# A two-layer recurrent decoder trunk: ScalarE rounds the weights of two input projections, two first tiles and two first chunks start in another order

## The chip, the cores and the metric

One NeuronCore of a Trainium2 chip runs the whole program. The metric is the device time of one execution in microseconds. Engines are called PE (TensorE), DVE (VectorE), ACT (ScalarE), POOL (GpSimd) and SP (SyncE, which here only issues DMAs).

## The reference

576 token columns (512 of a prompt, 8 samples of 8) pass through two layers with shared weights, all in float32, width 1024:

```python
h = rms_norm(x, norm_mix[l])
y, s = even_mixer(h, ...)  if l % 2 == 0 else odd_mixer(h, ...)   # z = h @ w_in ... y = concat @ w_out
x = x + y
h = rms_norm(x, norm_ffn[l])
y, c = conv_ffn(h, ...)          # u = h @ w_up; causal conv of 3; (val * silu(gate)) @ w_down
x = x + y
```

The even mixer projects to 30 tiles of 128 columns (16 for an mLSTM, 14 for an RWKV-7) and 8 gate columns; the odd mixer to 16 tiles (12 for gated linear attention, 4 for an S5 scan) and 16 gate columns. The feed-forward part has 44 tiles up and 22 x 128 rows down. Outputs are both token groups and all new states.

## The kernel before

**How a projection is computed.** Activations stay transposed, eight tiles k of 128 x 576. Every matrix product in float32 is made of three passes with operands rounded to the fast float32 format: high x high, high x low, low x high (`mm3`). A tile of output is 8 k x 2 halves of 288 columns x 3 passes = 48 matmuls. So each weight tile (128 x 1024) that a DMA brings into one of the two slots of `w_ring` has to be split: `w_hi` = rounded weight, `w_lo` = weight minus `w_hi`, both with two slots. A slot may be refilled with tile t+2 once PE has finished tile t (`proj_done`), and PE may start tile t+2 once it is split (`w_split`) and its PSUM pair has been read out (`FREE`). SP loads tile t+2 into `w_ring` when tile t is split.

**Who splits.** In both input projections (`e_in`, `o_in`), both output projections and both down projections POOL does both steps (`chunk`, L1327: a multiplication by ones, then a subtraction). In the two up projections (`ffn`) ACT makes the high half (L1962) and POOL only the subtraction. The activations are split by ACT (high, L1924) and DVE (low, L270 called from `low_sum`), with squares for the norm beside them, in `split_x`.

**Start.** PE computes the 36 gate columns (`small`) as each split tile k of x arrives, then the sum of squares over partitions (`norm`), then tile 0 of `e_in`. `norm` releases ACT's Ln and Exp that make `rstd`; every read-out of a tile (`evac`, `to_ext`, on DVE) multiplies by it. After `rstd`, ACT works on the gate rows (L2001 to L2005) and one exponential for the S5 part (L2007, its step size). DVE interleaves read-outs of tiles 0 to 15 with gate logs, running maxima, row logs and, after tile 5, `s5_angles` (both the sine and the cosine argument), after tile 7 `s5_coefficients`.

**Odd layer.** In `odd_dve` DVE reads out tiles 0 and 1, then for t = 0, 1 computes log decays, a scan and key differences (L1013 to L1020), and only then reads out tiles 2 and 3. In `odd_act` ACT does the gate functions; then, for 14 level masks, DVE's differences, ACT's Exp and DVE's scalings follow each other (`levels`), between the read-outs of tiles 4 to 15.

**Feed-forward.** Per tile: read-out by DVE, three conv taps (ACT, DVE, DVE), SiLU, product, high half, low half. POOL copies conv state in and out (`state_in`, `state_out`). `down` has, per output tile, three chunks of 8, 7 and 7 k in alternating slots. PE's first chunk (8 k) needs 14 low halves of the activations (`act_lo`), the second 15 and the third all 22. Before its first chunk POOL copies out the last conv state (it waits for the read-out of up tile 43) and, in layer 0, splits the 16 gate columns of the next layer (`wad`).

Each engine executes its instructions in the order written; the code order is the schedule.

Of the kernel before, what the change touches and what calls it, by code (L numbers as in the profile page):

```python
# [26 lines left out]
P = 128  # L27
# [4 lines left out]
TH = T // 2  # L32
# [143 lines left out]
def program(nc, d, o):  # L176

    ctx = ExitStack()
    with ctx:
# [702 lines left out]
        def odd_act(act, A, chain, norm, head_norm, split_h):  # L882
            norm(2)

# [19 lines left out]
            level_exps(0, 14)  # L904
# [64 lines left out]
        def odd_dve(dve, V, chain, evac, head_norm, split_h):  # L969
# [40 lines left out]
            for t in range(2):  # L1010
# [4 lines left out]
                chain(V.tensor_tensor_scan(b_, c_("scan128", T), la, 0.0, ALU.mult, ALU.add))  # L1015
                kd = KG[:, t, :]
# [4 lines left out]
            evac_z(2)  # L1021
            diffs(0)
            diffs(1)
            evac_z(3)
# [298 lines left out]
        def _(pool):  # L1323
# [22 lines left out]

            def ffn(l):
# [35 lines left out]
                for t in range(2 * FT):  # L1383
# [3 lines left out]
                    if t + 2 < 2 * FT:  # L1387
                        state_in(t + 2)

            def down(l):  # L1390
                pool.wait_ge(S("proj_done"), USE[f"down{l}"] - 1)
                pool.wait_ge(S("w_split"), CHUNK0[f"down{l}"])
                with pool.Fori(0, 4) as i:
                    chain.loop(i, 6)
# [8 lines left out]
                    chain.end_loop(4)  # L1403
# [17 lines left out]
            ffn(0)  # L1421
            pool.wait_ge(S("o_small_in"), 32)
            split(wad, wad_hi, wad_lo, S("small_split"))
            down(0)
            pool.wait_ge(S("chunk_used"), 17)
            project("o_in")
            pool.wait_ge(S("s5_y"), SP4)
            project("o_out")
            ffn(1)
            down(1)  # L1430
# [3 lines left out]
        def _(pe):  # L1434
# [7 lines left out]
            def small(name, out, hi, lo):  # L1442

                for k in range(KT):
# [5 lines left out]
                last.then_inc(S("gates_done"), 1)  # L1450

            def project(name, between=None, breaks=(), lead=0):
# [15 lines left out]
                for s in () if lead else range(2):  # L1468
# [443 lines left out]
        def _(act):  # L1912
            A = nc.scalar.activation
            chain = Chain(act, S("act_chain"))

            def split_x(n, name):

                for k in range(KT):
# [11 lines left out]
                    A(sq[:, k % 2, :], xT[:, k, :], ACT.Square).then_inc(S("sq_ready"), 1)  # L1930

# [926 lines left out]
```

## Time and profile before

| | us |
|---|---|
| median of 3 runs | 1760.52 (1759.35 to 1769.03) |
| span of the profiled execution | 1763.6 |
| PE busy | 1634.1 (93%) |
| DVE / POOL / ACT busy | 1053.1 / 875.7 / 471.8 |
| PE idle between matmuls, waiting for DVE arena L267 | 26.1 |
| ... for DVE hT_r L270 (low halves of x) | 18.2 |
| ... for POOL dual_r L267 (a split weight) | 16.2 |

The given time of an execution is that of the whole device run; of the profiled one only the span, 1763.6 us from its first to its last instruction, is given, and it lies 3.1 us above the median. `PE PP L280` is any matmul, `L267` any two-input elementwise operation, `L270` any scalar_tensor_tensor: these are helper lines, so what an instruction is has to be read from its tiles and its place. A start and a duration stand at the head of a timeline row, in brackets the idle time of its engine just before it and what ended it. Matmuls overlap, so their durations (0.29 at full clock, 0.43 at half) are longer than the distance of their starts.

### The profile page before, as it was taken

How to read it: one execution, taken by the hardware profiler on the slowest of the kernel's cores; microseconds unless marked ns; L12 is line 12 of the kernel's file. 1: busy time of each engine (PE TensorE's matmuls, PEld its weight loads, DVE VectorE, ACT ScalarE, POOL GpSimd, SP SyncE). 2: the span in 40 equal slices, each digit the busy share in tenths (PEclk: the TensorE clock that was granted, in tenths of full speed). 3: DMA queues.
4: the chain of work that ended last, by engine and by line, in shares of the span. 5: the costliest groups of instructions: out<-in, count | busy, mean ns of one | idle time of the engine just before them, and what ended most of it. 6: DMA issues, size and time to landing. Idle time of an engine off the chain costs nothing. (4 is left out here: it accounts for less than half of the span.)

```text
span 1763.6 us, 35383 instructions
## 1 busy us (share of the span) xinstructions
PE 1634.1 (93%) x14910; PEld 1576.0 (89%) x14910; DVE 1053.1 (60%) x1533; ACT 471.8 (27%) x688; POOL 875.7 (50%) x731
## 2 busy tenths in 40 slices
PE   6999996588998999999989998999899999998996
PEld 5999985487987999999989998977799999998996
DVE  4816768747645777776632239676676777765012
ACT  4002123610133343333310031132414333332001
POOL 4666688094013644444376656700374444445763
PEclk8999988688999999999999999998999999999998
DMA  4222111021052222222222222274332222222222
GB/s 176 84 71 83 60 74 54 1 75 56 13 200 69 90 84 83 83 83 83 72 66 88 76 79 60 71 210 139 91 98 77 84 83 83 84 83 61 81 83 88
DMA packets 50679, 149.09 MB, mean 85 GB/s; under 512 B 17552, under 2 KB 19232, under 8 KB 48416
## 3 DMA queue, kind: packets, MB, share of 16 engines
q1 hardware_dynamic: 50592, 147.91, 26.3%
q8 instruction: 58, 0.95, 0.2%
q14 instruction: 29, 0.24, 0.0%
HBM read 127.58 MB, written 19.13 MB: 83 GB/s over the span
## 5 line engine op out<-in xcount | busy, mean ns | idle before, releaser
L280 PE MATMUL PP<-arena_r,dual_r 128*128 128x288 f32 (+1 forms) x6428 | 1116.9, 298 | 39.9 <-POOL dual_r L267 16.2
L280 PEld LDWEIGHTS PP<-arena_r,dual_r 128*128 128x128 f32 (+1 forms) x6428 | 965.3, 190 | 44.3 <-POOL dual_r L267 13.9
L280 PE MATMUL PP<-hT_r,dual_r 128*128 128x288 f32 (+1 forms) x2176 | 647.7, 298 | 0.0
L267 POOL TENSOR_TENSOR dual_r<-w_ring,dual_r 128x1024 fp32r<-128x1024 f32 (+1 forms) x198 | 485.1, 2450 | 17.7 <-ACT dual_r L1962 4.6
L267 POOL TENSOR_TENSOR dual_r<-w_ring,cst 128x1024 fp32r<-128x1024 f32 (+1 forms) x114 | 216.7, 1901 | 408.6 <-PE PP L280 262.2
L280 PEld LDWEIGHTS PP<-hT_r,dual_r 128*128 128x128 f32 (+1 forms) x2176 | 410.5, 189 | 1.3
L270 DVE SCALAR_TENSOR_TENSOR rowbuf<-rowbuf,convp 128x592 f32<-128x592 f32 x176 | 271.3, 1542 | 91.3 <-ACT rowbuf L1985 90.7
L280 PE MATMUL PP<-arena 64*64 64x64 f32 (+6 forms) x3640 | 206.0, 256 | 37.1 <-DVE arena L267 15.3
L280 PEld LDWEIGHTS PP<-arena 64*64 64x64 f32 (+2 forms) x3640 | 182.8, 148 | 57.9 <-issue 32.6
L1962 ACT ACTIVATE dual_r<-w_ring 128x1024 fp32r<-128x1024 f32 x84 | 89.2, 1062 | 332.1 <-PE PP L280 332.1
L267 DVE TENSOR_TENSOR xT<-PP,xT 128x576 f32<-128x576 f32 x32 | 24.2, 758 | 255.5 <-PE PP L280 255.5
L267 DVE TENSOR_TENSOR rowbuf<-PP,rstd 128x288 f32<-128x288 f32 (+2 forms) x306 | 90.5, 351 | 109.0 <-PE PP L280 97.6
L267 DVE TENSOR_TENSOR arena<-arena 128x256 f32<-128x256 f32 (+12 forms) x168 | 128.9, 800 | 6.9 <-ACT arena L1953 3.7
L280 PE MATMUL PP<-rowbuf_r,dual_r 128*128 128x288 f32 (+1 forms) x544 | 112.4, 301 | 7.0 <-DVE arena L267 6.3
L1365 POOL COPY rowbuf<-arena 128x16 f32<-128x16 f32 x88 | 19.7, 226 | 173.4 <-DVE rowbuf L270 173.4
L280 PEld LDWEIGHTS PP<-rowbuf_r,dual_r 128*128 128x128 f32 (+1 forms) x544 | 88.4, 189 | 9.1 <-DVE arena L267 6.5
L1372 POOL COPY arena<-rowbuf 128x18 f32<-128x18 f32 x88 | 17.6, 200 | 139.0 <-DVE rowbuf L267 139.0
L1985 ACT ACTIVATE rowbuf<-rowbuf,convp 128x592 f32<-128x592 f32 x88 | 76.4, 868 | 24.8 <-DVE rowbuf L267 24.8
L267 DVE TENSOR_TENSOR arena<-PP,rstd 128x576 f32<-128x576 f32 (+2 forms) x28 | 21.1, 753 | 88.5 <-PE PP L280 78.7
L267 DVE TENSOR_TENSOR rstd<-rstd,sq 128x576 f32<-128x576 f32 x35 | 73.2, 2091 | 0.1
L267 DVE TENSOR_TENSOR arena<-arena,PP 128x128 f32<-128x128 f32 (+4 forms) x114 | 35.3, 311 | 50.9 <-PE PP L280 41.4
L280 PE MATMUL PP<-dual_r 128*128 128x288 f32 (+1 forms) x244 | 58.9, 297 | 1.9 <-DVE hT_r L270 1.9
(266 smaller groups left out, 1348.9 us busy)
## 6 DMA issues: line engine op xcount, KB each, us to landing
w_ring<-in_w SPq DMA_DIRECT2D x150, 512.0 KB, 3.5
w_ring<-in_w_down SPq DMA_DIRECT2D x32, 448.0 KB, 3.3
w_ring<-in_w_down SPq DMA_DIRECT2D x16, 512.0 KB, 3.5
xT<-in_x SPq DMA_DIRECT2D x8, 576.0 KB, 7.1
gy_scratch<-dual SPq DMA_DIRECT2D x1, 2304.0 KB, 7.0
dual<-gy_scratch SPq DMA_DIRECT2D x1, 2304.0 KB, 13.7
out_y<-hT SPq DMA_DIRECT2D x4, 576.0 KB
xT<-in_C SPq DMA_DIRECT2D x1, 2064.0 KB, 9.2
```

The lines of the kernel that those rows point to most:

```text
L267: return eng.tensor_tensor(out, a, b, op)
L270: return nc.vector.scalar_tensor_tensor(out=out, in0=a, scalar=s, in1=b, op0=op0, op1=op1)
L280: return nc.tensor.matmul(out, lhsT, rhs, start=start, stop=stop)
L1365: G.tensor_copy(samp[:, :, 0:2], convin[:, t, :].rearrange("p (j n) -> p j n", j=8)).then_inc(S("conv_in"), 1)
L1372: G.tensor_copy(convout[:, t, :].rearrange("p (j n) -> p j n", j=9), last2).then_inc(S("conv_out"), 1)
L1962: A(w_hi[:, t % 2, :], w_ring[:, t % 2, :], ACT.Copy).then_inc(S("w_hi"), 1)
L1985: A(cv[:, i % 2, s, 0:NCV - 2], ext[:, s, 0:NCV - 2], ACT.Identity, bias=convp[:, l, p0 + 3:p0 + 4], scale=convp[:, l, p0:p0 + 1]).then_in ...
```

## The change

The whole change, by place:

- **Start.** POOL no longer makes the high halves of weight tiles 0 and 1; ACT does, after the squares of x tiles 5 and 6. PE computes the gate columns for k = 0 to 4, then waits for tile 0's split and computes tile 0 for k = 0 to 4, then alternates gate columns and tile 0 for k = 5, 6, 7, then `norm`.
- **ScalarE's high halves.** For `e_in` (all 30 tiles) and `o_in` (tiles 2 to 15) ACT copies `w_ring` to `w_hi` (`high`) and POOL only subtracts (`project_low`). The calls to `high` are placed in ACT's order: tiles 2 to 9 after the S5 step exponential, 10 to 13 after the sines, and so on.
- **Moved orders.** `s5_angles` in two parts, after tiles 5 and 6. In the odd layer the read-outs of tiles 2 and 3 move into the gate loop, between scan and key differences; ACT does both Exp before both Ln. POOL starts the first chunk of `down` before the last conv state is copied out, and splits `wad` between chunks 1 and 2.

```diff
-        def odd_act(act, A, chain, norm, head_norm, split_h):
+        def odd_act(act, A, chain, norm, high, head_norm, split_h):
             norm(2)
+            high("o_in", "o_hi", 2)
...
             for t in range(2):
-                chain(A(BC[:, t, :], BC[:, t, :], ACT.Exp, scale=-1.0))
+                last = A(BC[:, t, :], BC[:, t, :], ACT.Exp, scale=-1.0)
+            chain(last)
+            for t in range(2):
                 A(BC[:, t, :], BC[:, t, :], ACT.Ln, bias=1.0).then_inc(S("gl_sp"), 1)
+            high("o_in", "o_hi", 3)
             for t in range(2):
+                high("o_in", "o_hi", 4 + t)
                 act.wait_ge(S("gl_kd"), t + 1)
...
-            level_exps(0, 14)
+            for k0, k1, js in ((0, 2, (6,)), (2, 4, (7,)), (4, 6, (8,)), (6, 8, (9,)), (8, 9, (10, 11, 12, 13)),
+                               (9, 11, (14,)), (11, 13, (15,)), (13, 14, ())):
+                level_exps(k0, k1)
+                for j in js:
+                    high("o_in", "o_hi", j)
...
                 chain(V.tensor_tensor_scan(b_, c_("scan128", T), la, 0.0, ALU.mult, ALU.add))
+                evac_z(2 + t)
                 kd = KG[:, t, :]
...
-            evac_z(2)
             diffs(0)
             diffs(1)
-            evac_z(3)
...
+            def project_low(name, sem, ahead=0):
+                first_chunks = 2
+                if name == "o_in":
+                    for s in range(first_chunks):
+                        pool.wait_ge(WL[s], 16 * (CHUNK0[name] // 2 + 1))
+                        pool.wait_ge(S("proj_done"), USE[name] + s - 1)
+                        chunk(s)
+                with pool.Fori(1, RUNS[name][1] // 2) as i:
+                    for s in range(2):
+                        pool.wait_ge(S(sem), 2 * i + (s - 1 + ahead))
+                        tt(G, w_lo[:, s, :], w_ring[:, s, :], w_hi[:, s, :], ALU.subtract).then_inc(S("w_split"), 1)
...
-                for t in range(2 * FT):
+                for t in range(2 * FT - 1):
                     state_out(t)
...
+                return lambda: state_out(2 * FT - 1)
-            def down(l):
+            def down(l, last_state, between=None):
+                c0 = CHUNK0[f"down{l}"]
                 pool.wait_ge(S("proj_done"), USE[f"down{l}"] - 1)
-                pool.wait_ge(S("w_split"), CHUNK0[f"down{l}"])
-                with pool.Fori(0, 4) as i:
-                    chain.loop(i, 6)
+                for e in range(6):
+                    tile, j = e // 3, e % 3
+                    pool.wait_ge(WL[e % 2], 16 * (c0 // 2 + e // 2 + 1))
+                    if e == 2 and between is not None:
+                        between()
+                    if e == 1:
+                        last_state()
+                        pool.wait_ge(S("proj_done"), USE[f"down{l}"])
+                    elif j == 1:
+                        pool.wait_ge(S("proj_done"), USE[f"down{l}"] + tile)
+                    elif e:
+                        pool.wait_ge(S("chunk_used"), 16 * l + 2 * tile + (j == 2) + 1)
+                    chunk(e % 2, DCH[j][1] * P)
+                with pool.Fori(1, 4) as i:
...
-            for s in range(2):
-                pool.wait_ge(WL[s], 16)
-                chunk(s)
-            project("e_in", 1)
+            for s in range(2):
+                pool.wait_ge(S("e_hi"), s + 1)
+                tt(G, w_lo[:, s, :], w_ring[:, s, :], w_hi[:, s, :], ALU.subtract).then_inc(S("w_split"), 1)
+            project_low("e_in", "e_hi", 2)
...
+            def first_tile(ks):
+                for k in ks:
+                    pe.wait_ge(S("h_lo"), k + 1)
+                    c = slice(k * P, (k + 1) * P)
+                    for a in range(2):
+                        h = slice(a * TH, (a + 1) * TH)
+                        last = mm3(PP[0][:, a, 0:TH], w_hi[:, 0, c], w_lo[:, 0, c], H_HI["e_in"][k][:, h],
+                                   H_LO["e_in"][k][:, h], k == 0, k == KT - 1)
+                if ks[-1] == KT - 1:
+                    last.then_inc(S("proj_done"), 1)
...
-            small("e_in", PP[2][0:36], wif_hi, wif_lo)
+            small("e_in", PP[2][0:36], wif_hi, wif_lo, range(5))
+            pe.wait_ge(S("w_split"), 1)
+            pe.wait_ge(FREE[0], 1)
+            first_tile(range(5))
+            for k in range(5, KT):
+                small("e_in", PP[2][0:36], wif_hi, wif_lo, range(k, k + 1))
+                first_tile(range(k, k + 1))
             norm(0)
-            project("e_in", None, {11: mlstm_columns})
+            project("e_in", None, {11: mlstm_columns}, done=1)
...
+            def high(name, sem, j):
+                act.wait_ge(WL[j % 2], 16 * ((CHUNK0[name] + j) // 2 + 1))
+                if USE[name] + j >= 2:
+                    act.wait_ge(S("proj_done"), USE[name] + j - 1)
+                A(w_hi[:, j % 2, :], w_ring[:, j % 2, :], ACT.Copy).then_inc(S(sem), 1)
...
                     A(sq[:, k % 2, :], xT[:, k, :], ACT.Square).then_inc(S("sq_ready"), 1)
+                    if n == 0 and k in (5, 6):
+                        high("e_in", "e_hi", k - 5)
...
             A(t_s, l_st, ACT.Exp).then_inc(S("s5_trig"), 1)
+            for j in range(2, 10):
+                high("e_in", "e_hi", j)
             act.wait_ge(S("o_rows"), 1)
...
             A(t_c, t_c, ACT.Sin).then_inc(S("s5_trig"), 1)
+            for j in range(10, 14):
+                high("e_in", "e_hi", j)
             for j in range(12, 16):
+                high("e_in", "e_hi", j + 2)
...
             for k in range(14):
                 s = k % 2
+                if k < 12:
+                    high("e_in", "e_hi", 18 + k)
...
-                    if j == 5:
-                        s5_angles()
+                    if j in (5, 6):
+                        s5_angles(j - 5)
```

## Rows read from the trace of the kernel before

**Rows 1.** The page's table of engines: busy time, share of the span, instructions.
```profile
PE 1634.1 (93%) x14910; PEld 1576.0 (89%) x14910; DVE 1053.1 (60%) x1533; ACT 471.8 (27%) x688; POOL 875.7 (50%) x731
```
**Rows 2.** PE's waits by releaser: us in total, times, longest.
```profile
PE PP L280 <- DVE arena L267: 26.1, 8, 7.0
PE PP L280 <- DVE hT_r L270: 18.2, 7, 8.5
PE PP L280 <- POOL dual_r L267: 16.2, 4, 7.4
```
**Rows 3.** Timeline of the start, 0 to 40 us: splits, their rivals, and PE's restarts.
```profile
11.57 0.81 DVE L270 SCALAR_TENSOR_TENSOR hT_r<-xT,vec,arena_r 128x576 fp32r<-128x576 f32 x1
12.68 2.13 POOL L267 TENSOR_TENSOR dual_r<-w_ring,cst 128x1024 fp32r<-128x1024 f32 x1 [5.01 <-DMA w_ring<-in_w]
12.97 2.45 DVE L270 SCALAR_TENSOR_TENSOR hT_r<-xT,vec,arena_r 128x576 fp32r<-128x576 f32 x1
20.67 0.45 PE L280 MATMUL PP<-arena_r,dual_r 128*36 128x288 f32 x1 [3.54 <-DVE hT_r L270]
25.51 0.75 DVE L267 TENSOR_TENSOR rstd<-rstd,sq 128x576 f32<-128x576 f32 x1
29.17 0.65 ACT L1935 ACTIVATE rstd<-PP 128x576 f32<-128x576 f32 x1 [3.69 <-PE PP L280]
39.01 0.23 ACT L2007 ACTIVATE rowbuf<-rowbuf 128x32 f32<-128x32 f32 x1
41.95 0.76 DVE L267 TENSOR_TENSOR arena<-PP,rstd 128x576 f32<-128x576 f32 x1 [5.64 <-PE PP L280]
48.32 0.76 DVE L267 TENSOR_TENSOR arena<-PP,rstd 128x576 f32<-128x576 f32 x1 [5.60 <-PE PP L280]
```
**Rows 4.** Stretches: PE, PEld, DVE, ACT, POOL busy (instructions), PE clock, DMA share, GB/s.
```profile
15.40:21.90 6.50, 2.88 (x12) 1.80 (x12) 6.50 (x4) 1.35 (x2) 6.42 (x3) 0.50 0.77 285
83.20:91.40 8.20, 8.14 (x50) 8.15 (x51) 4.50 (x19) 2.52 (x4) 1.75 (x1) 0.79 0.21 64
1075.60:1084.30 8.70, 8.69 (x50) 8.69 (x51) 5.02 (x14) 1.84 (x4) 0.00 (x0) 0.74 0.21 61
889.30:897.30 8.00, 7.91 (x49) 7.91 (x50) 8.00 (x8) 3.14 (x6) 4.77 (x3) 0.80 0.42 122
```
**Rows 5.** The two steps of a weight split on POOL, and ACT's high half.
```profile
35.60 1.90 POOL L267 TENSOR_TENSOR dual_r<-w_ring,cst 128x1024 fp32r<-128x1024 f32 x1 [12.76 <-PE PP L280]
37.57 2.40 POOL L267 TENSOR_TENSOR dual_r<-w_ring,dual_r 128x1024 fp32r<-128x1024 f32 x1
L1962 ACT ACTIVATE dual_r<-w_ring x84: 1057/1062/1063, 606.0 to 1586.4; 128x1024 fp32r<-128x1024 f32 x84
```
**Rows 6.** Timeline around PE's stop before tile 8 of the even layer.
```profile
82.46 1.41 DVE L270 SCALAR_TENSOR_TENSOR arena<-PP,rstd 128x576 f32<-128x576 f32 x2
83.25 0.43 PE L280 MATMUL PP<-arena_r,dual_r 128*128 128x288 f32 x1 [2.80 <-DVE arena L270]
```
**Rows 7.** Timeline of the odd layer's input projection: DVE, and PE's restart at tile 4.
```profile
1063.20 4.62 DVE L267 TENSOR_TENSOR arena<-arena 128x512 f32<-128x512 f32 x2
1075.61 0.61 PE L280 MATMUL PP<-rowbuf_r,dual_r 128*128 128x288 f32 x1 [6.30 <-DVE arena L267]
1100.06 8.40 DVE L267 TENSOR_TENSOR arena<-arena 128x288 f32<-128x288 f32 x8
1148.95 0.82 DVE L267 TENSOR_TENSOR arena<-arena 128x288 f32<-128x288 f32 x2
```
**Rows 8.** Timeline between up and down projection, layer 0, and PE's restart in layer 1.
```profile
883.90 3.22 DVE L270 SCALAR_TENSOR_TENSOR rowbuf<-rowbuf,convp 128x592 f32<-128x592 f32 x2 [0.95 <-ACT rowbuf L1985]
891.43 8.83 DVE L267 TENSOR_TENSOR arena_r<-arena,arena_r 128x576 fp32r<-128x576 f32 x8
889.39 110.86 PE L280 MATMUL PP<-arena_r,dual_r 128*128 128x288 f32 x819 [7.36 <-POOL dual_r L267]
1605.24 142.84 PE L280 MATMUL PP<-arena_r,dual_r 128*128 128x288 f32 x1056 [6.11 <-POOL dual_r L267]
```

More of the change, by code:

```diff
@@ L1402, in down @@
                         chunk(e % 2, DCH[j][1] * P)
[L1403 removed]
+                    chain.end_loop(3)
             pool.sem_inc(S("chunk_used"), 1)
@@ L1420, in _, with small_weights @@
             project("e_out")
[L1421 to L1424, printed above, removed]
+            last_state = ffn(0)
+            def small_weights():
+                pool.wait_ge(S("o_small_in"), 32)
+                split(wad, wad_hi, wad_lo, S("small_split"))
+            down(0, last_state, small_weights)
             pool.wait_ge(S("chunk_used"), 17)
-            project("o_in")
+            project_low("o_in", "o_hi")
             pool.wait_ge(S("s5_y"), SP4)
             project("o_out")
-            ffn(1)
-            down(1)
+            down(1, ffn(1))
         @block.tensor
@@ L1440, in norm, with small @@
                 last.then_inc(S("sq_summed"), 1)
-            def small(name, out, hi, lo):
-                for k in range(KT):
+            def small(name, out, hi, lo, ks=range(KT)):
+                for k in ks:
                     pe.wait_ge(S("h_lo"), 8 * SPLIT[name] + k + 1)
@@ L1449, in small, with project @@
                                    k == 0, k == KT - 1)
-                last.then_inc(S("gates_done"), 1)
-            def project(name, between=None, breaks=(), lead=0):
+                if ks[-1] == KT - 1:
+                    last.then_inc(S("gates_done"), 1)
+            def first_tile(ks):
+                for k in ks:
+                    pe.wait_ge(S("h_lo"), k + 1)
[4 more added lines that the diff above has]
+                                   H_LO["e_in"][k][:, h], k == 0, k == KT - 1)
+                if ks[-1] == KT - 1:
+                    last.then_inc(S("proj_done"), 1)
+            def project(name, between=None, breaks=(), lead=0, done=0):
                 n = RUNS[name][1]
@@ L1467, in project @@
                             last.then_inc(S("proj_done"), 1)
-                for s in () if lead else range(2):
+                for s in () if lead else range(done, 2):
                     pe.wait_ge(S("w_split"), CHUNK0[name] + s + 1)
@@ L2210, in _ @@
             split_x(2, "o_in")
-            odd_act(act, A, chain, norm, head_norm, split_h)
+            odd_act(act, A, chain, norm, high, head_norm, split_h)
             split_x(3, "ffn1")
@@ L2367, in row_logs, with s5_angles @@
                 V.tensor_copy(r_mo[:, 1:9], m_s).then_inc(S("ml_rows"), 1)
-            def s5_angles():
-                dve.wait_ge(S("s5_trig"), 1)
-                chain(tt(V, t_a, l_re, t_s, ALU.mult))
-                chain(tt(V, t_b, l_im, t_s, ALU.mult))
-                for out, shift in ((t_s, 0.0), (t_c, np.pi / 2)):
+            def s5_angles(part):
+                if part == 0:
+                    dve.wait_ge(S("s5_trig"), 1)
+                    chain(tt(V, t_a, l_re, t_s, ALU.mult))
+                    chain(tt(V, t_b, l_im, t_s, ALU.mult))
+                for out, shift in (((t_s, 0.0),) if part == 0 else ((t_c, np.pi / 2),)):
                     chain(V.tensor_scalar(t_n, t_b, 1.0 / TWO_PI, shift / TWO_PI, ALU.mult, ALU.add))
```

1 line of the change is left out of this document (added).

## The prediction

> **What bounds the kernel now.** First the table of engines: PE is busy 93% of the span, the others at most 60% [rows 1]. So time is saved only where PE stands idle or runs at the lower of its two clock levels. Second, PE's waits by releaser: only three groups have to do with what is edited, DVE's read-outs and masks (26.1 us), the low halves of x (18.2) and split weights from POOL (16.2) [rows 2]. Third, the timeline around each restart, which gives the places: the start, tile 8 of the even layer (2.80 us idle), tile 4 of the odd layer (6.30), and the first chunk of either down projection (7.36 and 6.11) [rows 3, 6 to 8]. Fourth, the granted clock of the stretch behind each restart: a tile that needs 6.37 us in steady state (read-outs at 41.95 and 48.32, [rows 3]) takes 8.1 to 8.7 us behind a stop, at a mean clock of 0.74 to 0.80 [rows 4]. A stop therefore costs its idle time and about 1.9 us more.
>
> A tile's split is 1.90 + 2.40 us on POOL [rows 5], below 6.37, so in steady state it is hidden before and after. With ACT's 1.06 for the high half, the path from a finished tile to the split becomes 1.06 + 2.40 = 3.5 us instead of 4.3: worth nothing by itself. ACT must get to it in time, though: everything queued ahead of it in ACT's order now stands ahead of PE's tile.
>
> **POOL and DVE.** A low half of x takes DVE 0.81 us; the one at 12.97, issued behind POOL's 2.13 us at 12.68, took 2.45 and ended 0.6 us after POOL did [rows 3]. DVE is held until POOL's instruction ends. Read-outs from PSUM stay at 0.76 with POOL at work. The Trainium skill, "SBUF — State Buffer", section "Who interferes with whom", says the same: two SBUF inputs on DVE and a reading GpSimd instruction exclude each other for the whole instruction, one SBUF input does not. By that rule an earlier POOL chunk only moves DVE's delay; without it both down projections would gain their whole idle time. The trace agrees with the rule.
>
> **The start.** POOL's first instruction on weights now waits for ACT. ACT needs 1.3 to 1.4 us per k; high half 0 falls at about 14.2 to 15.3, POOL subtracts until 18.0 (2.75 us with DVE beside it), high half 1 until 17.8, POOL until 20.6. DVE is held for two POOL instructions instead of four: the last square is summed at about 22.6 instead of 26.3 (25.51 + 0.75, [rows 3]). PE has computed gates 0 to 4 by 15, idles until 18.0, and is at half clock then, as between 15.4 and 21.9 now [rows 4]. It has 30 + 36 matmuls left, 0.133 us apart at full clock (6.37 / 48), 0.24 at half. At half clock for about 4 us (some 17), then 49 x 0.133: it ends at 28.6, `norm` behind it. ACT's Ln starts at about 29.8 against 29.17 [rows 3]: the gates are no earlier, but tile 0 is finished too, a full tile ahead.
>
> What is late next is tile 2. Its high half stands behind the gate rows and the S5 exponential: that ends at 39.24 now [rows 3], some 39.9 then. Plus 1.06 and 2.40: split at 43.4. Tile 1 ends at about 36, so PE idles over 7 us and starts tile 2 at 43.4; before it started at 41.9, when tile 1 was finished. So +1.5 us, and +1.9 for the lower clock: the gain is given back, **+3.4**. Bounds: tile 2 released at once by ACT would be a tile early, -6; a walk wholly at half clock (66 x 0.24 = 16 us) makes the chain 5 us later, +9.
>
> **s5_angles in two.** Read-out 6 came at 82.46, behind both parts, and PE waited 2.80 for it [rows 6], plus 1.9 clock: **-4.7**. With half of it behind tile 7, and PE 3.4 us later anyway, both read-outs fall within their 6.4 us. The coefficients now wait on ACT (high half 9, a table load, the sines) and push read-out 8 by 3 us at most, still within a tile. Even layer: -1.3. Later highs stand one per tile beside a read-out; the squares after tile 25 (3 us) fit too. POOL reaches the S5 work up to 1 us earlier; I cost that at 0, +-1.5.
>
> **Odd layer.** Tile 4 waited 6.30 us because read-out 2 stood behind both scans and key differences (4.62 of the latter were mostly POOL's hold) [rows 7]; the tile then took 8.7 at clock 0.74 [rows 4]. After the move read-out 2 follows the first scan, at 1063, just as tile 2 ends; read-out 3 at 1069.3. High halves 4 and 5 are ready at tile end + 3.5. PE goes on without a stop: 6.30 + 8.7 - 6.4 = **-8.6**. DVE is then about 2 us behind PE instead of ahead; its next cover is POOL's shorter turn. Eight mask operations took 8.40 us with POOL in the way and would take 4 x 0.82 = 3.3 free [rows 7]; with one 2.4 hold per tile, 5.7 + 0.75, just PE's pace. High halves 7, 8, 9 come behind mask exponentials and keep, by this account, 1 to 2.5 us of slack. The saved table loads on ACT are hidden behind tile 1. Bounds: 0 if the lag grows into new stops, -8.6 - 1.
>
> **Down projections.** Layer 0: chunk 0 is split from 876.9 to 881.3, before tile 43 ends at 882.0: the 7.36 stop goes. What is late next is the second chunk: it needs `act_lo` 15, and that comes by DVE, two taps (3.22), ACT's SiLU, the product, then the low halves (from 891.43, 8.83 for eight) [rows 8]. Now POOL's chunk 0 holds tile 42's taps and delays read-out 43 by 1 us, chunk 1 (884.3 to 888.5) holds the taps, chunk 2 the product. I get the 15th low half at 894.6. PE has finished chunk 0 by 888.4, stops 6.2 us, and runs chunk 1 partly at half clock until 902.1; it ended at 902.9 before (897.3 + 42 x 0.133). **-0.9**. Layer 1, without the gate split: **-1.1**. Bounds for both together: 0, and, if DVE were not held, 7.36 + 6.11 + 2 x 1.7 = -17.
>
> **Sum.** +3.4 - 4.7 - 8.6 - 0.9 - 1.1 = -11.9 on the span of 1763.6. The span lies 3.1 above the median of the runs; the same difference on 1760.5 gives **1748.6 us**.
>
> **Rivals.**
> A. *The down projections gain most of their stop* (low halves come in time). For: the first chunk's wait is truly on POOL. Against: the chain of holds above. Another -7: 1741.5.
> B. *Half of the odd layer's gain is eaten by new small stops.* For: slack of 1 us at high halves 8 and 9. Against: POOL's hold per tile falls from 4.3 to 2.4. +4.5: 1753.
> C. *The start is worse*: PE stays at half clock, since the walk starts from idle. +5: 1753.5.
> D. *Slower: high halves late in ACT's queue.* In the odd layer each stands behind Exps that wait for DVE's differences, which are held by POOL. Should DVE lag 2 us more than I find, highs 7, 8, 9, 14 and 15 are each 2 us late, each with 1.9 us of lower clock: 5 x 3.9 = 19.5, hence 1768. It decides from a DVE lag of about 4 us at tile 6. Against: before, with POOL's longer turns, DVE caught up by tile 9.
>
> **Chances.** Forecast 0.55 (own range 1744 to 1752), A 0.15, B 0.13, C 0.10, D 0.04, others 0.03. A measurement of this kernel can tell about 0.5% (8.8 us) from no change. Faster by more: the forecast but for its upper edge (0.52), A, and a few of B and C (0.07): 0.74. Within: 0.22. Slower: 0.04. Range 1739 to 1755.
>
> **What the profile after would show.** PE idle 6 to 8 us before tile 2 of the even layer, released by POOL, with ACT's gate rows ahead of the high half; no stop at tile 8; none at tile 4 of the odd layer, input projection there 8 to 9 us shorter; in both down projections the stop moved behind 48 matmuls, released by DVE's `arena_r`, 5 to 6 us long. Wrong if tile 2 starts before 42, if the stop before the second chunk is absent, or if new stops appear among odd tiles 7 to 15.

## The result, and the profile after

The changed kernel takes 1752.2 us (median of 7 runs, 1749.19 to 1757.59) against 1766.7 for the kernel before on the same chip (7 runs, 1758.65 to 1769.03). The ratio is 0.9939 [0.9920, 0.9957]: 0.61% or some 11 us faster. (The two medians lie 14.4 us apart, because the seven runs before fall into three at 1758.65 to 1760.52 and four at 1766.65 to 1769.03; the two means lie 11.1 us apart.) The interval reaches from 0.43% to 0.80%, across the 0.5% mark, so a gain of more than 0.5%, to which the prediction gave 0.74, is likely but not shown. The forecast, 1748.6 from a base of 1760.5, was a gain of 0.68%; 1752.2 lies in its range. The size was nearly right. Two of the reasons were not, as the experiments show.

The after page's engine table, to be read beside [rows 1]: PE's share is still 93%, VectorE is busy 1009.9 us and POOL 785.8, and ScalarE has taken over part of POOL's work.

```profile
PE 1629.8 (93%) x14910; PEld 1573.0 (90%) x14910; DVE 1009.9 (58%) x1533; ACT 513.0 (29%) x730; POOL 785.8 (45%) x687
```

PE's waits by releaser (what PE waited for: us in total, times, longest) answer to [rows 2]:

```profile
PE PP L280 <- DVE arena L267: 19.4, 7, 6.8
PE PP L280 <- POOL dual_r L267: 13.3, 4, 7.2
PE PP L280 <- DVE arena_r L267: 12.5, 3, 6.4
PE PP L280 <- DVE hT_r L270: 11.4, 5, 8.8
```

DVE's `arena` fell from 26.1 mostly by the 6.3 of the odd layer's tile 4, and the 2.8 of L270 (tile 8, even layer) is gone. `hT_r` fell from 18.2. POOL's 16.2 became 13.3, but with other contents: the two stops before the down projections (7.36 and 6.11, [rows 8]) left the group, and stops at the start came in (3.30 and 7.22). The down stops now stand as `arena_r`, up from 1.9 to 12.5. These are the three restarts in the timeline of PE (start, us, instruction, count, idle before and its releaser), at tile 0, at tile 2 and in the first down projection:

```profile
18.37 0.51 PE L280 MATMUL PP<-arena_r,dual_r 128*128 128x288 f32 x1 [3.30 <-POOL dual_r L267]
...
43.49 0.60 PE L280 MATMUL PP<-arena_r,dual_r 128*128 128x288 f32 x1 [7.22 <-POOL dual_r L267]
...
890.79 4.42 PE L280 MATMUL PP<-arena_r,dual_r 128*128 128x288 f32 x17 [6.36 <-DVE arena_r L267]
```

The stretches behind them, in the windows view (window, its length, busy us and count of PE, PEld, DVE, ACT, POOL, then granted clock, DMA share, GB/s): tile 2 of the even layer runs at a clock of 0.65, then tiles 3 to 8 of the even layer and the first tiles of the odd one at 1.00 without a gap.

```profile
43.00:52.00 9.00, 8.51 (x44) 8.52 (x45) 0.00 (x0) 0.00 (x0) 2.68 (x2) 0.65 0.39 117
52.70:92.00 39.30, 39.30 (x298) 39.30 (x298) 29.78 (x63) 9.16 (x11) 14.59 (x6) 1.00 0.27 81
1051.00:1071.80 20.80, 20.80 (x160) 20.80 (x159) 19.46 (x26) 9.10 (x11) 7.92 (x4) 1.00 0.26 77
```

The same two stretches of the kernel before, cut at the same read-outs:

```profile
48.30:91.40 43.10, 40.16 (x290) 39.72 (x290) 37.89 (x62) 3.14 (x5) 27.49 (x12) 0.96 0.26 82
1056.60:1084.30 27.70, 21.40 (x147) 21.17 (x146) 23.77 (x26) 5.73 (x8) 14.64 (x6) 0.88 0.20 58
```

The row to look at is POOL's: 27.49 us and 12 instructions became 14.59 and 6, and DVE, with one more instruction, is busy 29.78 us instead of 37.89. DVE's work did not shrink; the time for which its instructions were held did.

To compare kernels whose early parts shift all later ones, every profile was cut at the starts of the same VectorE read-outs. The first column is when the gate columns are read out, the first use of `rstd`; "to tile 2" goes from there to read-out 2; "up to down" goes from the read-out of the last up tile to the first read-out of the down projection. In us, granted clock in brackets:

| kernel | rstd read | to tile 2 | tiles 2 to 9 | odd tiles 1 to 15 | up to down, layer 0 | layer 1 |
|---|---|---|---|---|---|---|
| before | 31.9 | 16.4 (1.00) | 49.5 (0.97) | 97.5 | 26.6 | 25.7 |
| after | 32.7 | 20.1 (0.74) | 44.5 (1.00) | 88.95 | 25.5 | 23.8 |
| change | +0.8 | +3.7 | -5.0 | -8.6 | -1.1 | -1.9 |

That is 12.1 us. The two spans (1763.6 and 1747.4) differ by 16.2. Between the even layer's last read-out and the first read-out of its output projection (231.19 to 555.55 in before), where nothing is edited, after needs 317.9 us and before 324.4; the profiles of the twelve other kernels have 318.4 to 326.7 for the same work. And one stretch in the even layer went the other way by 3.0 (last section). So profile against profile overstates the change, and the stages are needed to see it. The stages scatter too: seven kernels (after, e1, e2, e4, e5, e9, e10) have the same down projections, and in their profiles the layer 0 stretch takes 25.2 to 25.6 us, the layer 1 stretch 23.8 (after) to 25.0 (e10). Against before that is -0.7 to -1.9 for layer 1, so the -1.9 of the table lies at the favourable end.

### The profile page after: what moved, and what is told of

It reads as the page before. It is cut to its first block, busy times and chain, and to the rows that moved or that the text cites. A ratio compares the mean times of both kernels' runs of the same rounds, so it can differ in the third digit from the quotient of the medians.

```text
span 1747.4 us, 35327 instructions
## 1 busy us (share of the span) xinstructions
PE 1629.8 (93%) x14910; PEld 1573.0 (90%) x14910; DVE 1009.9 (58%) x1533; ACT 513.0 (29%) x730; POOL 785.8 (45%) x687
## 4 chain that ended last, share of the span: by engine, by line
PE 82%; DVE 8%; issue 4%; ACT 2%; DMA 1%; POOL 1%; SPq 1%; DVEq 0%; ACTq 0%; POOLq 0%
PE PP L280 82%; DVE arena L267 3%; POOL dual_r L267 1%; DVE xT L267 1%; DMA w_ring<-in_w 1%; DVE rowbuf L270 1%; SPq L538 1%; DVE rstd L267 1%; DVE arena L270 0%; DVE hT_r L270 0%; DVE hT L267 0%; DMA y_scratch<-arena 0%; DVE hT L270 0%; PE PP L1744 0%; ACT arena L2237 0%
## 5 line engine op out<-in xcount | busy, mean ns | idle before, releaser
L280 PE MATMUL PP<-arena_r,dual_r 128*128 128x288 f32 (+1 forms) x6428 | 1118.6, 298 | 39.8 <-POOL dual_r L267 13.3
L270 DVE SCALAR_TENSOR_TENSOR rowbuf<-rowbuf,convp 128x592 f32<-128x592 f32 x176 | 273.7, 1555 | 91.4 <-ACT rowbuf L2049 90.7
L267 POOL TENSOR_TENSOR dual_r<-w_ring,cst 128x1024 fp32r<-128x1024 f32 (+1 forms) x70 | 127.9, 1828 | 291.4 <-PE PP L280 147.5
L280 PEld LDWEIGHTS PP<-arena 64*64 64x64 f32 (+2 forms) x3640 | 179.3, 146 | 57.5 <-issue 30.9
L2026 ACT ACTIVATE dual_r<-w_ring 128x1024 fp32r<-128x1024 f32 x84 | 89.2, 1062 | 332.1 <-PE PP L280 332.1
L267 DVE TENSOR_TENSOR arena<-arena 128x256 f32<-128x256 f32 (+12 forms) x168 | 109.2, 684 | 7.3 <-ACT arena L2017 3.7
L1976 ACT ACTIVATE dual_r<-w_ring 128x1024 fp32r<-128x1024 f32 x44 | 46.6, 1060 | 166.9 <-PE PP L280 166.9
```

The lines of the kernel that those rows point to most:

```text
L267: return eng.tensor_tensor(out, a, b, op)
L270: return nc.vector.scalar_tensor_tensor(out=out, in0=a, scalar=s, in1=b, op0=op0, op1=op1)
L280: return nc.tensor.matmul(out, lhsT, rhs, start=start, stop=stop)
L1976: A(w_hi[:, j % 2, :], w_ring[:, j % 2, :], ACT.Copy).then_inc(S(sem), 1)
L2026: A(w_hi[:, t % 2, :], w_ring[:, t % 2, :], ACT.Copy).then_inc(S("w_hi"), 1)
```

## The experiments

The prediction's account takes ScalarE's high halves as worth nothing by themselves and gives the gains in both input projections to the moved orders. The other account: the gains come from ScalarE's high halves, because VectorE is then held by one POOL instruction per tile instead of two. All times are medians and all ratios are to the kernel before on the same chip.

**e1: the walk undone.** Gates, sum of squares and tile 0 one after another again, all else as after.

```diff
-            first_tile(range(5))
-            for k in range(5, KT):
-                small(..., range(k, k + 1))
-                first_tile(range(k, k + 1))
-            norm(0)
-            project("e_in", None, {11: mlstm_columns}, done=1)
+            small("e_in", PP[2][0:36], wif_hi, wif_lo, range(KT))
+            norm(0)
+            project("e_in", None, {11: mlstm_columns})
```

> The changed kernel with TensorE's first instructions put back in the old order: all gate columns, the norm, then tile 0 alone; ScalarE's high halves stay. My theory: the walk over k is worth nothing, because tile 2 waits for its high half, which stands in ScalarE's queue behind the gate rows. In the old order the gate columns end at about 23 us and the norm at 24.5, some 5 us EARLIER than with the walk, so ScalarE ends its exponential for S5 at about 35 instead of 40.0 and tile 2's split is ready at about 38.4 instead of 43.5; tiles 0 and 1 fill TensorE from 24.5 to 39 (partly at half clock). Tile 2 then starts at 38 to 40, 4 to 5 us earlier than in the changed kernel: about 1748 us, 3 to 6 below it. Rival (the walk pays by itself, a tile of work placed into idle time): tile 2 starts 4 to 6 us later than 43.5, 1757.

1747.7 us, 0.9909 [0.9889, 0.9929]. Read-out 2 falls at 46.05 instead of 52.74: the walk costs 6.7 us at this place. ScalarE's queue and PE, from e1's timeline:

```profile
25.75 0.66 ACT L1993 ACTIVATE rstd<-PP 128x576 f32<-128x576 f32 x1 [6.01 <-PE PP L280]
...
35.74 1.04 ACT L1970 ACTIVATE dual_r<-w_ring 128x1024 fp32r<-128x1024 f32 x1
...
39.39 0.40 PE L280 MATMUL PP<-arena_r,dual_r 128*128 128x288 f32 x1 [0.72 <-POOL dual_r L267]
```

And in the kernel after:

```profile
29.92 0.65 ACT L1999 ACTIVATE rstd<-PP 128x576 f32<-128x576 f32 x1 [9.79 <-PE PP L280]
...
39.76 0.23 ACT L2071 ACTIVATE rowbuf<-rowbuf 128x32 f32<-128x32 f32 x1
39.89 1.99 ACT L1976 ACTIVATE dual_r<-w_ring 128x1024 fp32r<-128x1024 f32 x2
```

With the walk, `norm` comes behind tile 0, so ScalarE's Ln, its gate rows and then high half 2 all come 4 us later (39.89 against 35.74), and PE idles 7.22 us before tile 2 instead of 0.72. Without it the start is 2.3 us shorter than before (46.05 against 48.32 in [rows 3]).

**e2: both angle parts together again**, after tile 5.

```diff
-                    if j in (5, 6):
-                        s5_angles(j - 5)
+                    if j == 5:
+                        s5_angles(0)
+                        s5_angles(1)
```

> The changed kernel with both parts of the S5 angles behind tile 5 again. Theory: the split of the angles is worth nothing in the changed kernel, since tile 2 is late and everything behind it with it, and since GpSimd holds VectorE for half as long: read-out 6 ends at about 82 to 83, tile 8 is due at 84.5, no stop, 0 +- 1 us against the changed kernel in the stretch up to tile 9 (read-out 9 at 97.3 in both). Rival (my prediction's row for it): the stop of 2.8 us before tile 8 and 1.9 us of lower clock come back, read-out 9 at about 102.

1749.71 us, 0.9916 [0.9893, 0.9939]. Tiles 2 to 9 take 44.5 us at clock 1.00, as in after. Splitting the angles is worth nothing at this place; the 5.0 us there come from something else. Here tile 2 is late, though, which gives VectorE slack; e9 tests the same without that.

**e3: the moved read-outs alone**, on the kernel before (`evac_z` of tiles 2 and 3 inside the gate loop).

```diff
                 ...   # scan of gate t
+                evac_z(2 + t)
                 ...   # key differences of gate t
-            evac_z(2)
-            evac_z(3)
```

> The kernel before with only the read-outs of odd tiles 2 and 3 moved into the gate loop; GpSimd still makes both halves. Theory: the move alone removes the stop before tile 4 (6.3 + 2.3 us), the high halves on ScalarE have no part in it: the stretch from odd tile 1 to tile 15 shortens by 8 to 9 us, total -8.6 us or 0.5%. Rival: without ScalarE's high halves GpSimd holds VectorE twice per tile, the lag at the masks grows beyond a tile, and new stops at tiles 8 to 10 take back 3 to 8 us: total -1 to -5 us.

1759.4 us, 0.9992 [0.997, 1.0013], no difference that can be measured. In the trace odd tiles 1 to 15 take 94.2 us instead of 97.5: -3.3, not the -8.6 expected; the rival's -1 to -5 holds. Two stops are left among them, the longer of 3.5 us. PE's waits in that stretch (1020 to 1160 us):

```profile
PE PP L280 <- DVE arena L267: 4.0, 2, 3.5
```

**e4: the down projection's new order on POOL alone**, on the kernel before: chunk 0 before the last conv state, `wad` between chunks 1 and 2.

```diff
-                pool.wait_ge(S("w_split"), CHUNK0[f"down{l}"])
-                with pool.Fori(0, 4) as i:
+                for e in range(6):
+                    ...
+                    if e == 1:
+                        last_state()
+                        ...
+                    chunk(e % 2, DCH[j][1] * P)
+                with pool.Fori(1, 4) as i:
```

> The kernel before with only GpSimd's new order at the start of both down projections. Theory: the stop moves from the first chunk to the second, which waits for low halves of the activations: from the last up tile's read-out to the first read-out of the down projection 1 to 2 us less in each layer, total -2 to -3 us, hardly measurable. Rival: both stops go, -13 to -17 us.

1763.14 us, 1.0 [0.9984, 1.0015]. In its trace the stretches are 25.3 and 24.8 instead of 26.6 and 25.7, -1.3 and -0.9: near the predicted -0.9 and -1.1, and together too small for the runs to tell.

**e5: high halves 2 and 3 moved ahead** in ScalarE's order: 2 before the Ln that makes `rstd`, 3 before the gates' Ln.

```diff
+            high("e_in", "e_hi", 2)
             ...   # rstd
+            high("e_in", "e_hi", 3)
             ...   # gate rows
-            for j in range(2, 10):
+            for j in range(4, 10):
```

> The changed kernel with ScalarE's high half of tile 2 moved ahead of the norm's Ln (ScalarE idles there) and that of tile 3 ahead of the gates' Ln. Theory: tile 2's split was late only by its place in ScalarE's order. Tile 2 now starts right behind tile 1 at about 36.5 instead of 43.5 and at full clock, tile 3 waits up to 1.5 us: 8 to 10 us less at read-out 9, provided VectorE's row logs keep pace; total 1742 to 1745 us. Rival: VectorE's chain of gate and row logs becomes the bound (its 17 us of work between read-outs 2 and 5 start earlier by only part of it) and 3 us or less remain.

1744.37 us, 0.9897 [0.9878, 0.9915]. ScalarE's rows:

```profile
29.62 1.06 ACT L1976 ACTIVATE dual_r<-w_ring 128x1024 fp32r<-128x1024 f32 x1 [10.78 <-PE PP L280]
...
31.99 0.65 ACT L1999 ACTIVATE rstd<-PP 128x576 f32<-128x576 f32 x1
...
38.55 1.06 ACT L1976 ACTIVATE dual_r<-w_ring 128x1024 fp32r<-128x1024 f32 x1
```

The Ln that makes `rstd` is 2.1 us later than in after, since high half 2 (which has to wait for tile 0's buffer) stands ahead of it. Yet tile 2 is read out at 43.28, 9.5 us earlier than in after: the stop of 7.22 us and the half clock behind it are gone. The time came out as expected (1742 to 1745). What held the walk back was a place in ScalarE's queue. Tile 2 is also 2.8 us ahead of e1's; the high halves moved without the walk were not run, so what the walk itself is worth with them is open.

**e6: POOL hardly splits the first three chunks of the down projections**, so that next to nothing holds VectorE there. It leaves out the split of all but 16 columns of each of these chunks.

```diff
-                    chunk(e % 2, DCH[j][1] * P)
+                    chunk(e % 2, 16 if e < 3 else DCH[j][1] * P)
```

> Leaves out nearly all of the weight split of the first three chunks of both down projections (16 of 1024 or 896 columns are split), otherwise the changed kernel. Theory: GpSimd's splits hold VectorE and so delay the low halves that the second chunk waits for. Without them the 15th low half comes at read-out 43 plus 0.9 (ScalarE's tap) + 1.6 (two taps) + 0.7 (SiLU) + 1.0 (product) + 0.75, about 6 us behind the end of the up projection instead of 12: the first chunk (6.4 us) covers it and the stop before the second chunk vanishes (0 to 0.5 us instead of 6.3), 6 to 8 us less per layer. Rival: the chain of VectorE and ScalarE sets the stop by itself: it stays above 4 us.

1735.64 us, 0.9876 [0.9835, 0.9917]. Both stretches take 17.6 us at clock 1.00, -7.9 and -6.2 against after. VectorE's rows between up and down, in after:

```profile
880.73 4.25 DVE L270 SCALAR_TENSOR_TENSOR rowbuf<-rowbuf,convp 128x592 f32<-128x592 f32 x2 [0.95 <-ACT rowbuf L2049]
...
885.75 4.23 DVE L267 TENSOR_TENSOR arena<-rowbuf 128x512 f32<-128x512 f32 x2 [0.76 <-ACT rowbuf L2031]
...
889.90 5.42 DVE L267 TENSOR_TENSOR arena_r<-arena,arena_r 128x576 fp32r<-128x576 f32 x8
```

and in e6:

```profile
883.21 1.80 DVE L270 SCALAR_TENSOR_TENSOR rowbuf<-rowbuf,convp 128x592 f32<-128x592 f32 x2 [0.95 <-ACT rowbuf L2049]
...
885.78 0.83 DVE L267 TENSOR_TENSOR arena<-rowbuf 128x512 f32<-128x512 f32 x2 [0.77 <-ACT rowbuf L2031]
...
886.52 5.47 DVE L267 TENSOR_TENSOR arena_r<-arena,arena_r 128x576 fp32r<-128x576 f32 x8
```

Two taps take 1.80 instead of 4.25, the two products 0.83 instead of 4.23, the eight low halves the same 5.4: in after POOL's chunks 1 and 2 lie over the taps and the products, and the low halves come behind them. Nothing was taken from PE's or ScalarE's work, and the stop before the second chunk is gone: it came from the hold.

**e7: PE waits per k in the last chunk of the first tile**, and that chunk is the larger one.

```diff
-DCH = ((0, 8), (8, 7), (15, 7))
+DCH = ((0, 7), (7, 7), (14, 8))
 ...
+                                    if a == 0 and k0 + nk > AHEAD and k > k0:
+                                        pe.wait_ge(S("act_lo"), FT * l + k + 1)
```

> The changed kernel with down chunks of 7, 7 and 8 k instead of 8, 7, 7, and with TensorE waiting for each low half k by itself in the third chunk. Theory: only the last 8 activations are late; two chunks (11.2 us) now need none of them, and the third can start with the 15th low half: no stop of 6 us, per layer 4 to 6 us less, total about 1742. Rival: the low halves are so late that TensorE trails them one by one and loses the same time at half clock: less than 1 us per layer.

1748.89 us, 0.9926 [0.9908, 0.9943]. Layer 0's stretch is 24.3 us (after 25.5), layer 1's 23.9 (23.8). One long stop became two short ones, and PE then kept running:

```profile
894.62 0.64 PE L280 MATMUL PP<-arena_r,dual_r 128*128 128x288 f32 x3 [2.58 <-DVE arena_r L267]
897.08 9.19 PE L280 MATMUL PP<-arena_r,dual_r 128*128 128x288 f32 x55 [1.83 <-DVE arena_r L267]
```

The idle time falls by some 2 us and the stretch by 1.2 at most, as the rival had it; 4 to 6 us per layer had been expected. The eight low halves, 5.42 us in after, take longer here, because POOL's next splits now lie over them:

```profile
892.20 8.84 DVE L267 TENSOR_TENSOR arena_r<-arena,arena_r 128x576 fp32r<-128x576 f32 x8
```

**e8: e5 and e7 together.**

```diff
 # e5's high halves 2 and 3, and e7's DCH and waits per k
```

> The two improvements of this call together (early high halves of tiles 2 and 3; down chunks 7, 7, 8 with a wait per k). They lie in different stretches, so they add: 1732 to 1738 us, 1.6% below the kernel before. If both rivals hold: within 4 us of the changed kernel.

1740.05 us, 0.9879 [0.9856, 0.9902]. Read-out 2 comes at 43.6, the down stretches are 24.7 and 24.1 us, against 25.5 and 24.8 in e5's profile. The 1732 to 1738 expected were missed, since e7's part brought less than 1 us per layer instead of 4 to 6.

**e9: e5 with the angles together**, a test of e2's answer where PE is 9 us earlier and read-outs have less slack.

```diff
 # e5's high halves 2 and 3, and e2's s5_angles(0); s5_angles(1) after tile 5
```

> e5 (tiles 2 and 3 split early, TensorE some 9 us ahead of the changed kernel) with both parts of the S5 angles behind tile 5 again. Theory: splitting the angles counts once the start is not late. VectorE's chain behind read-out 2 (gate logs, maxima, row logs, angles) then has no slack of 9 us: read-out 6 comes 2 to 5 us behind its tile's due time and tile 8 stops: the stretch from read-out 2 to read-out 9 takes 47 to 50 us instead of 44.5. Rival: GpSimd's shorter hold alone (one instruction per tile instead of two) frees VectorE, and the stretch stays at 44.5: the split of the angles is worth nothing anywhere.

1744.77 us, 0.9892 [0.987, 0.9915], like e5's 0.9897. Tiles 2 to 9 take 44.5 again, not the 47 to 50 expected: the rival holds. VectorE's read-outs about the angles, which are both done between 62.60 and 68.2:

```profile
61.93 0.74 DVE L270 SCALAR_TENSOR_TENSOR arena<-PP,rstd 128x576 f32<-128x576 f32 x1
...
68.16 0.75 DVE L270 SCALAR_TENSOR_TENSOR arena<-PP,rstd 128x576 f32<-128x576 f32 x1
...
74.04 0.76 DVE L270 SCALAR_TENSOR_TENSOR arena<-PP,rstd 128x576 f32<-128x576 f32 x1 [5.13 <-PE PP L280]
```

Both parts fit between two read-outs 6.2 us apart, and at the next one VectorE waits 5.13 us for PE. Before, the read-out behind them came at 82.46 and kept PE waiting 2.80 us [rows 6]. What the hold costs is seen on five small VectorE products just ahead of the angles. In before, where both POOL instructions of a tile lie over them (67.51 to 72.76):

```profile
67.38 5.53 DVE L267 TENSOR_TENSOR arena<-arena 4x512 f32<-4x512 f32 x5
```

and in e9, where no POOL instruction does:

```profile
60.23 1.63 DVE L267 TENSOR_TENSOR arena<-arena 4x512 f32<-4x512 f32 x5
```

Of what is edited in this stretch, the split angles are out of account by e2 and e9, and the late tile 2 by e9. That leaves ScalarE's high halves. They were not run alone on the kernel before, so this is by elimination.

**e10: the read-outs moved back**, in the kernel after: ScalarE's high halves without the move. This and e3 are the two halves of the odd layer's change.

```diff
-                evac_z(2 + t)
+            evac_z(2)
             ...   # key differences of gate 1
+            evac_z(3)
```

> The changed kernel with the read-outs of odd tiles 2 and 3 behind the gate loop again, ScalarE's high halves kept. Read-out 1 to 15 took 97.5 us before, 88.9 in the changed kernel, 94.2 with the move alone. Theory: the shorter hold makes the gate loop about 3 us shorter, but read-out 2 still stands behind it and behind ScalarE's exponentials' inputs; tile 4 stops for 3 to 5 us and runs at half clock: 94 to 96 us, so the two edits give 1.5 to 4 and 3.3, and together more than their sum. There is one more danger: the high half of tile 4 and 5 stand ahead of the key exponentials, which wait for nothing new. Rival: ScalarE's high halves alone bring the whole gain: 89 to 90 us.

1753.01 us, 0.994 [0.9919, 0.9961], the ratio of after (0.9939). Odd tiles 1 to 15 take 88.9 us, which is after's own number (before 97.5, e3 94.2); 94 to 96 were expected, and the rival's 89 to 90 holds. Its windows row has no gap and full clock:

```profile
1052.00:1073.00 21.00, 21.00 (x161) 21.00 (x160) 17.88 (x24) 8.50 (x12) 8.32 (x3) 1.00 0.21 57
```

VectorE's timeline, in the order of before:

```profile
1056.28 2.54 DVE L1023 TENSOR_SCALAR arena<-arena 128x576 f32<-128x576 f32 x1
...
1060.24 0.83 DVE L267 TENSOR_TENSOR arena<-arena 128x512 f32<-128x512 f32 x2
...
1061.77 0.46 DVE L1023 TENSOR_SCALAR arena<-arena 128x576 f32<-128x576 f32 x1
...
1063.66 2.84 DVE L267 TENSOR_TENSOR arena<-arena 128x512 f32<-128x512 f32 x2
1066.43 0.74 DVE L267 TENSOR_TENSOR arena<-PP,rstd 128x576 f32<-128x576 f32 x1
```

The first pair of key differences, 4.62 us in [rows 7], takes 0.83, the second 2.84, and read-out 2 follows at 1066.43, in time for tile 4, which before was released by it with 6.30 us lost. From read-out 1 to read-out 2 VectorE works through the same instructions in 11.6 us here and in 18.2 before. In neither trace does it wait for ScalarE on the way, so the other edit left in e10, both Exp ahead of both Ln, is not what made this faster. In after, with the move, read-out 2 stands ahead of the key differences, and VectorE waited 1.04 us for PE there; that is slack which tile 4 does not need:

```profile
1057.47 0.76 DVE L267 TENSOR_TENSOR arena<-PP,rstd 128x576 f32<-128x576 f32 x1 [1.04 <-PE PP L280]
1058.15 3.01 DVE L267 TENSOR_TENSOR arena<-arena 128x512 f32<-128x512 f32 x2
```

**e11: ScalarE also makes the high halves of the down projections' first two chunks** (on e5); POOL only subtracts there.

```diff
+                    if e < 2:
+                        pool.wait_ge(S("w_hi"), 2 * FT * l + 2 * FT - 1 + e)
+                        tt(G, w_lo[:, e, 0:m], w_ring[:, e, 0:m], w_hi[:, e, 0:m], ALU.subtract)
+                        continue
 ...
+                    A(w_hi[:, t % 2, 0:m], w_ring[:, t % 2, 0:m], ACT.Copy)   # for t = 44, 45 too
```

> e5 and, in both down projections, the high halves of the first two chunks made by ScalarE, as it does for the up tiles; GpSimd only subtracts there. Theory (VectorE's hold sets the stop before the second chunk): two of GpSimd's instructions fall away that stood before VectorE's taps and product, so the 15th low half comes some 4 us earlier, the stop falls from 5.5 to 6.4 us to 2 to 3, and each layer gains 3 to 5 us: total about 1736 to 1738, 7 below e5. Rival: the third chunk, which needs all 22 low halves and whose two instructions still hold VectorE, takes the gain back: 0 to 2 us per layer.

1750.21 us (1750.05 without one execution of 3149 us, see the last section), 0.9917 [0.9898, 0.9936]; its down stretches are 27.2 and 27.4 us, 1.7 and 2.6 worse than e5's.

```profile
874.44 12.70 DVE L267 TENSOR_TENSOR arena_r<-arena,arena_r 128x576 fp32r<-128x576 f32 x8
...
881.31 2.40 POOL L267 TENSOR_TENSOR dual_r<-w_ring,cst 128x1024 fp32r<-128x1024 f32 x1 [1.97 <-PE PP L280]
...
887.28 7.99 PE L280 MATMUL PP<-arena_r,dual_r 128*128 128x288 f32 x42 [6.12 <-DVE arena_r L267]
```

The taps and products are less held, but POOL, done sooner, starts its next split while the eight low halves run: these take 12.70 us instead of 5.42, and the stop only moved. Here a faster cover engine made the bound one later. Neither the 3 to 5 us per layer expected nor the rival's 0 to 2 came.

**e12: e11 and e7 together.**

```diff
 # e11's high halves for chunks 0 and 1, and e7's DCH and waits per k
```

> e11 with the chunks of 7, 7 and 8 k and a wait per k in the third (the edit of e7). Theory: with fewer holds the low halves come at 0.75 us each from about 6 us after the up projection's end, the first two chunks (11.2 us) cover them all, no stop above 1 us is left: 6 to 8 us less per layer than in e5, about 1731. Rival: as in e7, GpSimd's split of the third chunk and of the next tile's first falls exactly among the low halves, and TensorE trails them: no better than e11.

1742.37 us, 0.9868 [0.9847, 0.9888], against before the best ratio of all; e8's 0.9879 lies within its interval, so e12 isn't shown to beat e8. Both beat the kernel after. The expected 1731 was not reached. The down stretches are 23.9 and 23.8; the first stop is the shortest found:

```profile
885.22 0.82 PE L280 MATMUL PP<-arena_r,dual_r 128*128 128x288 f32 x3 [1.48 <-DVE arena_r L267]
```

With waits per k, PE follows the low halves as they come, and so e11's long series of them no longer shows: the stretches are no longer than e8's 24.7 and 24.1.

## Why the prediction was right and wrong

**The start: mechanism right, the clock term too small.** Ln at 29.92 (forecast 29.8), tile 2 at 43.49 (43.4), released by POOL behind high half 2 at 39.89, after 7.22 us idle. Tile 2 then took 9.25 us where the prediction had 6.4 + 1.9: a stop of 7 us with a restart at half clock cost 2.9, so +4.4 at read-out 2 instead of +3.4. e1 splits it further: the walk costs 6.7 us, and without it the start is 2.3 us shorter than before. The prediction saw the earlier end of the squares, let the walk use it up ("the gates are no earlier"), and did not price the start without the walk.

**`s5_angles` in two, -4.7: size right, cause wrong.** Tiles 2 to 9 lost 5.0 us, but e2 and e9 keep all of it with the angles together. The step that failed is the one on ScalarE's high half: "the path from a finished tile to the split becomes 1.06 + 2.40 = 3.5 us instead of 4.3: worth nothing by itself". It priced the high half by PE's path to the next tile alone. The same prediction had the rule for the other path: VectorE is held until POOL's instruction ends. With one POOL instruction per tile instead of two, VectorE is held less (five products in 1.63 us instead of 5.53), and in e2 and e9 its read-outs are in time without any moved part; in e9 VectorE waits 5.13 us for PE at the second read-out behind the angles.

**The odd layer, -8.6: size exact (97.5 to 88.95), cause wrong, by the same step.** The prediction gave all of it to the moved read-outs and the shorter hold came only as "its next cover". e10 has the gain whole without the move; e3 has 3.3 of it from the move alone. The two overlap: the move alone leaves a stop of up to 3.5 us, the shorter hold alone leaves none. That both terms came out near their forecast sizes was luck: each was priced as the whole of a stop, and another edit removed that stop.

**The down projections, -0.9 and -1.1: right.** The stop went behind 48 matmuls, to the second chunk, released by `arena_r`, 6.36 and 5.47 us (forecast 6.2), for -1.1 and -1.9; e4 alone gives -1.3 and -0.9. (For layer 0 the prediction's own figures, 902.9 and 902.1, give -0.8; that is within the scatter.) The account by holds was what sized it, and e6 shows the hold to be the cause: 14.1 us for both layers with it gone, near the bound of -17 minus the 3 already had. The Trainium skill, "SBUF — State Buffer", section "Who interferes with whom", excludes two SBUF inputs on VectorE and a reading GpSimd instruction from each other; e6's two products, 4.23 us with POOL at work and 0.83 without, agree. The prediction's "one SBUF input does not" leaves out an exception of the same section: by it `tensor_scalar` can run in a mode that uses both of VectorE's port pairs, and is then excluded as well. This case agrees: in e10 the instruction at L1023, a `tensor_scalar` with one tensor input, takes 2.54 us the first time and 0.46 the second, and the first lies under this POOL instruction:

```profile
1056.02 2.47 POOL L267 TENSOR_TENSOR dual_r<-w_ring,dual_r 128x1024 fp32r<-128x1024 f32 x1 [7.85 <-ACT dual_r L1977]
```

The same instruction takes 2.54 and 0.46 us in before. No term of the sum hung on the exception.

**The rivals.** A, B and D did not happen: the down stop stayed, no new stops came in odd tiles 7 to 15, and high halves were late nowhere but at tile 2. C did not happen either: the walk ended as forecast (Ln at 29.92 for 29.8), and the 1.0 us that the start cost beyond the forecast came behind the stop at tile 2.

**The sum and the base.** The touched stretches give -12.1 against -11.9. The time was off by 3.6 us for another reason. "The span lies 3.1 above the median" was taken as what lies around the span. It isn't: in all runs whose span is on record the time is the span + 1.7 to 1.9 us, so the profiled execution was by that a run of some 1765.4 us, near the 1766.7 of the fuller sample, while the median of three (1760.52) lay low in runs that spread from 1758.65 to 1769.03. From its own execution's time the same sum gives 1763.6 - 11.9 + 1.8 = 1753.5, 1.3 above the measured 1752.2.

What stays open: the ratio of after carries 0.0018, some 3.3 us, of uncertainty to either side, so that no single part below that is told by times, only by the stages of single profiles. It is also open whether both Exp ahead of both Ln in the odd layer is worth anything by itself, and ScalarE's high halves were not run alone on the kernel before. And 6.4 us of the difference of the two spans lies in work that is the same in both; these are taken as scatter because the other profiles scatter there too, not because a cause was found.

## What to carry to other kernels

When an engine is only cover (busy, but off the critical path), price it by whom it holds, and not only by the path it is on: halving the instructions of POOL beside a busy VectorE was worth 5.0 and 8.6 us here, while moved read-outs and split work in the same places were worth nothing more. An instruction in an in-order queue is bound by its place there: two high halves moved ahead gave 9.5 us at tile 2, where the walk without them had cost 6.7. Before crediting a gain to a moved instruction, undo that one part with the rest in place, as well as doing it alone; here e3 alone would have given the move 3.3 of the 8.6 us, and e10 shows that it adds nothing once the hold is shorter.

## What the runs showed of the hardware

**A stretch with small matmuls lost its full clock without idle time, and by a varying amount.** The stretch with `mlstm_columns` (fp32 matmuls of a few columns, between read-outs 21 and 22) took 12.5 us in before, e2, e6, e7 and e10, 14.0 in e1, e3, e4, e5, e8 and e9, and 15.5 in after, e11 and e12, whatever was edited: three values, 1.5 us apart. The 30 smallest matmuls (4x4) took 3.60 us in before and 5.42 in after. The windows of 170 to 190 us, in before:

```profile
170.00:190.00 20.00, 20.00 (x144) 19.73 (x144) 11.70 (x21) 1.57 (x2) 10.30 (x5) 0.91 0.17 53
```

in after:

```profile
170.00:190.00 20.00, 20.00 (x122) 19.73 (x121) 6.87 (x19) 2.56 (x3) 3.59 (x2) 0.74 0.18 53
```

and in e2:

```profile
170.00:190.00 20.00, 20.00 (x145) 19.73 (x144) 9.86 (x23) 3.47 (x4) 6.02 (x3) 0.91 0.18 53
```

PE is busy 20.00 us in each, at 0.91, 0.74 and 0.91. That it is the small matmuls is argued from the place, not tested: no run has them moved or left out.

**The time of a run goes roughly with its clock.** The runs of after were 1749.19 and 1750.39 us at 0.956, 1751.51 and 1754.90 at 0.955, 1752.22 and 1754.11 at 0.953, and 1757.59 at 0.949. That is 8 us between runs of one kernel, as much as most parts of this change are worth; the order is not strict, and which of the two drives the other is not shown.

**What a restart costs is not set by the length of the stop.** Against 6.4 us in steady state, the tile behind 2.80 us of idle time took 8.2, behind 6.30 us 8.7, behind 7.36 us 8.0 [rows 4, 6 to 8], and behind the 7.22 us in after 9.25. So 1.6 to 2.9 us come on top, in no order that the idle time gives. In layer 1 the same stop of 5.47 us stands in after and in e5, and the stretch around it takes 23.8 and 24.8 us.

**One execution took 3149.14 us,** of e11, whose five others lay between 1746.01 and 1755.78; its recorded clock is 1.0, no trace shows it, and its cause is not known.
